# Moving the context stream's front and attention of the second block into the expert loop of layer 1

## The chip, the cores and the metric

The kernel runs on one core of a Trainium2 chip. The metric is device time in microseconds (us) of one execution. All arithmetic is fp32.

## The reference, cut to what matters

Two networks run one after the other on 256 tokens of width 1024.

```
first_block(x):   for layer in (0, 1):
    x += g1 * attention(norm(x))            # layer 0 differential, layer 1 stick-breaking
    x += g2 * moe(norm(x))                  # 32 experts of 1024 -> 512 -> 1024, top 2 of 8 in the top group
    then final norm
second_block(x, ctx):   y = ctx; for l in (0, 1):
    for each stream s in (y, x):            # context stream y, main stream x
        f, gate, u, v, gate, c_q, c_kv, k_rope, a_gate = split(norm_mod(s) @ w_in[l])   # 2208 columns
        fourier branch, spatial gate branch, low-rank q, k, v with norms of heads (rope for x)
    x += gate * (concat(f, g, attend(q_x, [k_y, k_x], [v_y, v_x]) * silu(a_x)) @ w_out[l])
    if l == 0:  y += gate_c * (concat(f, g, attend(q_y, k_y, v_y) * silu(a_y)) @ w_out[l])
```

The second block's context stream of layer 0 does not depend on the first block at all; only stream x does. The four passes of the second block are numbered p = 0 (context, l = 0), 1 (x, l = 0), 2 (context, l = 1, keys and values only), 3 (x, l = 1).

## The kernel before

Each engine has its own program, with the order written out by hand; semaphores tie them together.

**The ring.** Weights come through `ring`, six slots (`RING`) of 2 MB. Item n of one long list goes to slot n % 6. SyncE walks the list: it waits until the slot's earlier user is `free` and issues one transfer (L1318 to L1333; the last two experts in pieces, L1306 and L1311). For each expert these are gate, up and down, 2 MB each.

**The expert loop (`experts`, both layers).** For expert e TensorE computes gate and up of up to 64 gathered rows (32 instructions of 512 columns), then half of a gather for the quad of experts to come, waits for `hid`, turns it, does the second half of the gather, waits for `hidT` and computes `down` (16 instructions). ScalarE applies SiLU (L1643), frees gate and up, copies `hidT` (L1507), applies gain and shift to the gathered rows (L1591) and stores the result rows of the expert before. VectorE multiplies SiLU by up (L1928, `hid`) and scales `down`'s result (L1950, `out_ev`). PSUM banks 0 and 1 alternate for gate and up, 5 and 6 for `down`, 3 takes the gathers. At e = 28 (`TAIL`) every engine reads the fullest count and the last four experts' lists are turned; from there results are scattered by matmuls.

**What layer 1's loop already does for the context stream (p = 0).** Its rows are normed, turned at e = 3 and 4, and multiplied by the five sections of `w_in`, which come as ring items at e = 6, 11, 16, 21 and 26 (`Y0_AT`); each has two fills (one per tile of 128 tokens) into banks 4 and 7. Section "kv" is 160 columns wide, the other four are 512.

**The second block.** After the loop, `sp_second` on SyncE issues the first section for x, small weights and constants (L499, L531), further sections and the output weights (L528) into slots 0 and 1 in turn; slots 2 to 5 hold the second block's own tiles. TensorE (`pe_second`) turns x and works through 20 half fills of p = 1, and among them, by the list `X0_IN`, does the 15 steps of `front(0, j)` and the 20 of `attention(0, k)`. A front step is one of: turning the low-rank parts (`turn_c`), matmuls of a unit of q or k and v, turning a unit's heads, one of three Fourier steps, the spatial gate, turning the mixed parts. An attention step k computes scores of unit k (a head and a tile), turns the normed exponentials of unit k - 2, and every second step multiplies by v. ScalarE and VectorE have the same steps in the same order (copies, Sqrt, Exp; squares, norms, maxima). Then `Y0_OUT` goes through the output projection of p = 0 with `front(1, j)` among it.

Of the kernel before, what the change touches and what calls it, by code (L numbers as in the profile page):

```python
# [12 lines left out]

# [24 lines left out]
RING = 6  # L38
SLOT = KT * 512
# [93 lines left out]
def program(nc, a, out, sb, sem, ctx):  # L133
# [124 lines left out]
    y_rows = [h, carve(TT, D)]  # L258
# [3 lines left out]
    selw = work[:, 4416:5440].rearrange("p (e t k n) -> p e t k n", e=QUAD, t=TT, k=2)  # L262
# [24 lines left out]
    cut = Cut()  # L287
    g4, g4b, g4c, og, eg = (cut(TT, NG) for _ in range(5))
    e32, e32b, memb, place, spot, fits, share, share2 = (cut(TT, NX) for _ in range(8))
# [3 lines left out]
    row_of, w12, kept = (cut(2, TT) for _ in range(3))  # L293
# [3 lines left out]
    EARLY = (2, 1)  # L297
    L_BASE = [4, 12 + 3 * NX - EARLY[0]]
# [20 lines left out]
    def down_done(eng, l, e):  # L319

        down = expert_item(l, e, 2)
        eng.wait_ge(*((sem("early_used"), EARLY[0] * l + e + 1) if e < EARLY[l] else (free(down), down // RING + 1)))

    def gu_bank(e):

        return bank[0 if e >= TAIL else e % 2]

    def slot(n):
        return n % RING

    def loaded(eng, n):

        eng.wait_ge(sem(f"loaded{slot(n)}"), 16 * (n // RING + (slot(n) >= 4)))

# [31 lines left out]
    Y0_AT = (6, 11, 16, 21, 26)  # L366
    Y0_BANKS = (4, 7)
    tail = ring[:, 2:RING, :].rearrange("p r n -> p (r n)")
    t_at = [0]

    def cut2(*shape):
        n = int(np.prod(shape))
        t = tail[:, t_at[0]:t_at[0] + n]
        t_at[0] += n
        assert t_at[0] <= (RING - 2) * SLOT
        names = "abc"[:len(shape)]
        return t if len(shape) == 1 else t.rearrange(f"p ({' '.join(names)}) -> p {' '.join(names)}",
                                                     **dict(zip(names[1:], shape[1:])))

    y = cut2(TT, D)  # L380
    cst2 = cut2(CONST2_W)
    w_uq, w_ukv, w_fm, w_gs = cut2(2, 768), cut2(1024), cut2(2, 256), cut2(4, P)
    qa_g, kva_g, qn_g, kn_g, ln_g = cut2(256), cut2(P), cut2(A_QK), cut2(A_QK), cut2(HD)
    kT2 = cut2(A_HEADS, 2 * S)
    scratch = cut2(4608)
    tok = [scratch[:, 768 * k:768 * k + 768].rearrange("p (h e) -> p h e", h=A_HEADS) for k in range(2)]
    sqr = scratch[:, 1536:2304].rearrange("p (h e) -> p h e", h=A_HEADS)
    rot = scratch[:, 2304:2560].rearrange("p (h e) -> p h e", h=A_HEADS)
    AT = scratch[:, 2560:3584].rearrange("p (k c s) -> p k c s", k=2, c=2)
    FT = scratch[:, 3584:4096].rearrange("p (c s) -> p c s", c=2)  # L390
# [6 lines left out]
    qT2 = carve(A_HEADS, S)  # L397
    v2 = carve(2 * TT, A_HEADS, A_V)
    mixT = [carve(4, S), carve(4, S)]
    assert carve.at <= y_turn_at  # L400
    carve = Carver(y_turn_at)
    hT2 = carve(KT, S)
    y_raw = hT2.rearrange("p a b -> p (a b)").rearrange("p (t d) -> p t d", t=TT)
    cqT = carve(2, S)
    ckvT = carve(S)
    out_tmp = carve(2, 512)
# [3 lines left out]
    for name, w in CONST2_COLS:  # L410
        C2[name] = cst2[:, at:at + w]
        at += w
# [82 lines left out]
    X1_IN = share_steps([0] * 11 + [1, 1, 1, 1, 2, 2, 2, 1, 4])  # L495

    def small_weights(eng, l, name):

        put = lambda dst, src, s_: eng.dma_start(dst, src).then_inc(sem(s_), 16)  # L499
        put(w_uq, a["w_uq_2"][l].rearrange("(c p) n -> p c n", p=P), name)  # L500
        put(w_ukv, a["w_ukv_2"][l], name)
        put(w_fm, a["w_fmix_2"][l].rearrange("(c p) n -> p c n", p=P), name)
        put(w_gs, a["g_ws_2"][l].rearrange("h p q -> p h q"), name)
# [5 lines left out]
    def small_in(eng, p):  # L509

        eng.wait_ge(*((sem("pool_weights"), 128 + 160) if p >= 2 else (sem("small_in"), 176)))
# [6 lines left out]
    def sp_second(sp):  # L518
        last = expert_item(1, NX - 1, 2)
        sp.wait_ge(free(last), last // RING + 1)  # L520
        for r, (p, what) in enumerate(WEIGHTS2):
# [35 lines left out]
    def pool_second(pool):  # L557
        pool.wait_ge(sem("x_done"), 4)
        mod_row(pool, rows[:, 4, :], 0, 2, "gate_y_in")
        pool.wait_ge(sem("x_fin"), TT)  # L560
        mod_row(pool, rows[:, 3, :], 1, 2, "gate_x_in")
        pool.wait_ge(sem("h2"), every("h2", 1))
        norm_rows(pool, 2)
        pool.wait_ge(sem("f_out"), every("f_out", 1))
# [52 lines left out]
    def keep_warm(b, n):  # L617

        for _ in range(n):
            nc.tensor.matmul(bank[b][:, 0:S], ident, cst[:, 0:S], start=True, stop=True, skip_group_check=True)  # L620
# [13 lines left out]
    def take_turned(act, copy, p, ts, banks):  # L634

        for t in ts[::2]:
            act.wait_ge(sem("h2T_mm"), nth("h2T_mm", p, t // 2 + 1))
            if p % 2:
                gain, shift, _ = col_set[4 + p // 2]
                for k in (t, t + 1):  # L640
                    nc.scalar.activation(hT2[:, k, :], bank[banks[t // 2]][:, k % 2 * S:(k % 2 + 1) * S], ACT.Identity,
                                         scale=gain[:, k:k + 1], bias=shift[:, k:k + 1]).then_inc(sem("h2T"), 1)
# [118 lines left out]
    def act_second(act, link, copy):  # L761
# [88 lines left out]
        for t in range(TT):  # L850
            stream_rms(act, link, 1, t)
# [1585 lines left out]
```

## Time and profile before

| | us |
|---|---|
| median of 3 runs | 1889.09 |
| lowest, highest | 1888.32, 1898.73 |
| the profiled execution's own time | 1889.08 |
| its span, first to last instruction | 1887.3 |
| TensorE busy in the span | 1699.9 (90%) |
| mean granted TensorE clock | 0.964 of full speed |
| HBM read and written | 572.83 MB and 12.15 MB |

The profile is of one execution. Its time is compared with the median, and instants are us from the span's start. A busy TensorE row is not TensorE at its peak: matmuls overlap, and their ends are modelled, so the distance between starts is the better measure.

### The profile page before, as it was taken

Reading aid. Unit: us, or ns where it says so; the run is one execution under the profiler, and the core shown is the slowest. Engines: PE = TensorE matmul, PEld = TensorE weight load, DVE = VectorE, ACT = ScalarE, POOL = GpSimd, SP = SyncE. Lnnn points to the kernel's source line nnn. Section 1 sums busy time; section 2 is a strip of 40 time slices with the busy share of each in tenths; the row PEclk is TensorE's granted clock in tenths of the full one; section 3 lists DMA queues with packets and bytes.
Section 4 is the critical chain, followed back from the end, with each engine's and each line's share of the span. In section 5 each row is a group of like instructions: output and inputs, shape, how many; then the busy total and the mean of one; then the engine's idle time right before and its main releaser. Section 6 shows DMA issues by size and latency. Waiting matters only on the chain.

```text
span 1887.3 us, 18240 instructions
## 1 busy us (share of the span) xinstructions
PE 1699.9 (90%) x7421; PEld 848.5 (45%) x7421; DVE 489.5 (26%) x927; ACT 405.8 (22%) x909; POOL 96.1 (5%) x167
## 2 busy tenths in 40 slices
PE   5997999888988879989999899999989899899988
PEld 3833543333333325735544333333443556555564
DVE  1356210000001104234240000000102334653362
ACT  2025221111101102025221111011111334443351
POOL 1121000000000010122000000000000000100000
PEclk9998999999999989989999999999999899999999
DMA  9999379999999999987379999999998712213310
GB/s 350 360 356 397 143 279 424 423 423 422 422 422 421 422 416 398 347 335 240 148 273 421 422 420 422 419 416 416 418 419 344 272 59 90 86 64 114 123 57 23
DMA packets 122519, 586.30 MB, mean 311 GB/s; under 512 B 10290, under 2 KB 15482, under 8 KB 97848
## 3 DMA queue, kind: packets, MB, share of 16 engines
q1 hardware_dynamic: 99064, 491.94, 64.6%
q0 software_dynamic: 16192, 82.06, 11.7%
q10 hardware_dynamic: 7168, 11.02, 1.6%
q8 instruction: 62, 1.02, 0.2%
q14 instruction: 33, 0.27, 0.0%
HBM read 572.83 MB, written 12.15 MB: 310 GB/s over the span
## 4 chain that ended last, share of the span: by engine, by line
PE 58%; DMA 27%; DVE 6%; ACT 3%; SPq 3%; issue 3%; ACTq 0%; DVEq 0%
PE psum L2029 53%; DMA ring<-in_expert_w_up 21%; DMA ring<-in_diff_w_in 2%; DMA work<-in_ada_w 2%; SPq L1306 1%; PE psum L620 1%; DMA ring<-in_consts 1%; DMA work<-in_w_mod 1%; DVE small L967 1%; SPq L1327 1%; PE psum L2268 1%; PE psum L1097 1%; DVE work L1928 1%; DVE work L1720 1%; ACT work L1643 1%
## 5 line engine op out<-in xcount | busy, mean ns | idle before, releaser
L2029 PE MATMUL psum<-ring,work 128*64 128x512 f32 (+5 forms) x4432 | 1154.8, 576 | 78.1 <-DMA ring<-in_expert_w_up 63.6
L2029 PEld LDWEIGHTS psum<-ring,work 128*64 128x64 f32 (+2 forms) x4432 | 445.0, 153 | 703.2 <-issue 667.1
L2029 PE MATMUL psum<-work 128*128 128x192 f32 (+8 forms) x920 | 192.5, 376 | 6.9 <-DVE small L1780 2.2
L1928 DVE TENSOR_TENSOR work<-work,psum 128x256 f32<-128x256 f32 x64 | 27.0, 421 | 611.6 <-ACT work L1643 611.6
L2029 PEld LDWEIGHTS psum<-work 128*128 128x128 f32 (+2 forms) x920 | 130.7, 192 | 101.0 <-issue 80.9
L1643 ACT ACTIVATE work<-psum 128x256 f32<-128x256 f32 x64 | 24.6, 385 | 688.5 <-PE psum L2029 688.5
L2029 PE MATMUL psum<-work,ring 128*128 128x256 f32 (+1 forms) x728 | 161.2, 380 | 4.4 <-DMA ring<-in_diff_w_in 1.5
L2029 PEld LDWEIGHTS psum<-work,ring 128*128 128x128 f32 x728 | 136.0, 192 | 29.7 <-issue 7.1
L1507 ACT ACTIVATE work<-psum 128x256 f32<-128x256 f32 (+4 forms) x165 | 70.3, 439 | 222.1 <-PE psum L2029 69.1
L1950 DVE TENSOR_TENSOR work<-psum,rows 128x512 f32<-128x512 f32 x64 | 44.3, 692 | 272.1 <-PE psum L2029 272.0
L1720 DVE SCALAR_TENSOR_TENSOR work<-work,small 128x2048 f32<-128x2048 f32 x28 | 65.9, 2352 | 79.3 <-DMA work<-in_ada_w 78.8
L1507 ACT ACTIVATE ring<-psum 128x512 f32<-128x512 f32 (+3 forms) x82 | 49.9, 609 | 76.8 <-PE psum L2029 56.4
L1591 ACT ACTIVATE work<-psum,small 128x192 f32<-128x192 f32 x128 | 58.5, 507 | 23.7 <-PE psum L2029 23.7
L1469 POOL DMA_INDIRECT work<-expert_rows,picks x8 | 7.7, 963 | 882.1 <-DMA expert_rows<-work 880.3
L2268 PE MATMUL psum<-cst,work 128*128 128x128 f32 x128 | 28.0, 300 | 16.1 <-DVE work L1928 16.1
L620 PE MATMUL psum<-cst 128*128 128x256 f32 x166 | 42.0, 406 | 0.0
L967 DVE TENSOR_REDUCE small<-psum 128x1 f32<-128x512 f32 (+1 forms) x48 | 28.8, 600 | 47.4 <-PE psum L2029 47.2
L2029 PE MATMUL psum<-work,small 128*2 128x512 f32 (+1 forms) x256 | 37.3, 666 | 3.8 <-DMA work<-in_ada_w 2.0
L840 ACT ACTIVATE ring<-psum,small 128x512 f32<-128x512 f32 (+1 forms) x48 | 29.6, 617 | 41.8 <-DVE small L967 40.2
L1177 PE MATMUL psum<-cst,ring 128*128 128x128 f32 x160 | 27.3, 286 | 11.9 <-DVE ring L973 11.4
L620 PEld LDWEIGHTS psum<-cst 128*128 128x128 f32 x166 | 32.7, 204 | 11.4 <-issue 7.0
L2029 PE MATMUL psum<-work,cst 128*128 128x256 f32 (+4 forms) x152 | 26.9, 400 | 12.1 <-DVE work L1999 6.3
(256 smaller groups left out, 815.1 us busy)
## 6 DMA issues: line engine op xcount, KB each, us to landing
ring<-in_expert_w_gate SPq DMA_DIRECT2D x60, 2048.0 KB, 17.0
ring<-in_expert_w_up SPq DMA_DIRECT2D x60, 2048.0 KB, 21.2
ring<-in_expert_w_down SPq DMA_DIRECT2D x57, 2048.0 KB, 20.8
work<-in_ada_w POOLq DMA_DIRECT2D x40, 1024.0 KB, 8.0
ring<-in_w_in SPq DMA_DIRECT2D x12, 2048.0 KB, 9.0
work<-in_w_mod POOLq DMA_DIRECT2D x16, 1024.0 KB, 7.7
ring<-in_diff_w_in SPq DMA_DIRECT2D x6, 2048.0 KB, 38.1
ring<-in_sb_w_in SPq DMA_DIRECT2D x6, 2048.0 KB, 25.3
```

Source lines behind the costliest of these rows:

```text
L620: nc.tensor.matmul(bank[b][:, 0:S], ident, cst[:, 0:S], start=True, stop=True, skip_group_check=True)
L840: nc.scalar.activation(pe_[:, k % 3, 0:n * P], bank[4 + k % 3][:, 0:n * P], ACT.Exp, bias=nm2[:, k % 3:k % 3 + 1], accum_out=sm2[:, k % 4: ...
L967: V.tensor_reduce(nm2[:, k % 3:k % 3 + 1], bank[4 + k % 3][:, 0:n * P], AX.X, ALU.max, negate=True).then_inc(sem("a_max"), 1)
L1177: ins = T.transpose(bank[(7, 2)[u % 2]][:, j * P:(j + 1) * P], pe_[:, u % 3, j * P:(j + 1) * P], ident)
L1507: copy = lambda o_, i_: nc.scalar.activation(o_, i_, ACT.Copy)
L1591: ins = nc.scalar.activation(hS[:, c // QUAD % 2, t, 0:QUAD * LIST], bank[b][:, k * S:k * S + QUAD * LIST], ACT.Identity, scale=gain[:, t: ...
L1643: nc.scalar.activation(s_act, gu_bank(e)[:, 0:S], ACT.Silu).then_inc(sem("silu"), 1)
L1720: ins = V.scalar_tensor_tensor(now, now, cond[:, 0, t:t + 1], before, ALU.mult, ALU.add)
L1928: V.tensor_tensor(hid, s_act, gu_bank(e)[:, S:2 * S], ALU.mult).then_inc(sem("hid"), 1)
L1950: V.tensor_tensor(outb[:, e % 2, :], bank[5 + e % 2], gate2, ALU.mult).then_inc(sem("out_ev"), 1)
L2029: return T.matmul(out_, lhsT, rhs, start=start, stop=stop, skip_group_check=True)
L2268: ins = T.transpose(bank[2][:, j * P:(j + 1) * P], src[:, j * P:(j + 1) * P], ident)
```

## The change

- All 15 front steps and 20 attention steps of p = 0 leave the second block's first stage, and run in layer 1's expert loop from e = 9 on: one ahead of an expert's gate and up, one after its first half gather. On ScalarE and VectorE they stand at the matching places. For this the five sections come one after another at e = 4 to 8, and the turning of the context rows at e = 2 and 3.
- From expert 7 on the ring has five slots in turn, not six (`KEPT` = 1). The sixth holds the second block's small weights and constants, which POOL now loads in the loop once the slot is free, and not SyncE after it.
- PSUM: in layer 1 gate and up use bank 0 alone, `down` bank 5 alone (to e = 27), gathers bank 1; `down` of expert e waits for the scaling of e - 1. The steps use 3, 4, 6 and 7.
- The SiLU table is loaded again ahead of SiLU in each expert that may have steps (`y0_roots`).
- Tiles get other places; keys and values of the two streams are apart, so the scores of x are two matmuls of 256 columns, not one of 512.

```
+KEPT = 1
-    Y0_AT = (6, 11, 16, 21, 26)
+    Y0_AT = (4, 5, 6, 7, 8)
+    SPLIT_AT = 7
+    SPLIT = expert_item(1, SPLIT_AT, 0)
-    def gu_bank(e):
-        return bank[0 if e >= TAIL else e % 2]
+    def gu_bank(l, e):
+        return bank[0 if l or e >= TAIL else e % 2]
+    def down_bank(l, e):
+        return 5 + (0 if l and e < TAIL else e % 2)
     def slot(n):
-        return n % RING
+        return n % RING if n < SPLIT else (n - SPLIT) % (RING - KEPT)
+    def turn_of(n):
+        return sum(slot(m) == slot(n) for m in range(n))
-    FRONT = 15
-    X0_IN = share_steps([0, 1, 1, 1, 1, 1, 2, 2, 2, 2, 2, 3, 3, 3, 3, 3, 1, 1, 1, 1])
+    FRONT, ATTN = 15, 20
+    Y0_STEP0 = Y0_AT[-1] + 1
+    def y0_step(front, attention, e, half):
+        j = 2 * (e - Y0_STEP0) + half - 1
+        if 0 <= j < FRONT:
+            front(0, j)
+        elif FRONT <= j < FRONT + ATTN:
+            attention(0, j - FRONT)
+    def y0_roots(e):
+        return 0 <= 2 * (e - Y0_STEP0) < FRONT + ATTN + 2
...
 (sp_second)
             if r == 0:
-                small_weights(sp, 0, "small_in")
-                sp.dma_start(cst2, a["consts2"]).then_inc(sem("small_in"), 16)
+                mix_weights(sp, 1, "small_x")
...
 (pe_second; act_second and dve_second alike)
-        for n, js in enumerate(X0_IN):
+        for n in range(2 * len(fills(1))):
             in_half(1, n)
-            for j in js:
-                front(0, j) if j < FRONT else attention(0, j - FRONT)
...
 (gpsimd)
+                for n in range(SPLIT - RING, SPLIT):
+                    if slot(n) >= RING - KEPT:
+                        pool.wait_ge(free(n), turn_of(n) + 1)
+                small_weights(pool, 0, "small_in")
+                pool.dma_start(rope, a["consts2"][:, 0:ROPE_W]).then_inc(sem("small_in"), 16)
+                pool.dma_start(cst2, a["consts2"][:, ROPE_W:]).then_inc(sem("small_in"), 16)
...
 (scalar, experts)
+                if l:
+                    y0_step(front, attention, e, 0)
+                    if y0_roots(e):
+                        act.preload_act_table(ACT.Silu)
                 act.wait_ge(sem("gu"), EACH["gu"] * l + e + 1)
...
                 if 0 < e < TAIL:
                     store(l, e - 1)
+                if l and e == Y0_AT[-1]:
+                    c_root(act, link, 0)
+                    v_root(act, 0)
+                if l:
+                    y0_step(front, attention, e, 1)
...
 (vector, experts: half 0 ahead of the wait for SiLU, half 1 ahead of the scaling)
...
 (tensor, experts)
+                if l:
+                    y0_step(front, attention, e, 0)
                 if i == 0:
                     pe.wait_ge(sem("hS"), EACH["hS"] * l + QUAD * (q + 1))
...
-                    gather(sel[:, (q + 1) % 2], 2 * i, bank[3][:, 0:QUAD * LIST])
+                    gather(sel[:, (q + 1) % 2], 2 * i, bank[GATHER[l]][:, 0:QUAD * LIST])
+                if l:
+                    y0_step(front, attention, e, 1)
                 pe.wait_ge(sem("hid"), EACH["hid"] * l + e + 1)
...
-                if e >= 2:
+                if l and 0 < e <= TAIL:
+                    pe.wait_ge(sem("out_ev"), EACH["out_ev"] * l + e)
+                elif e >= 2:
                     pe.wait_ge(sem("out_ev"), EACH["out_ev"] * l + e - 1)
```

## Rows read from the trace of the kernel before

**Rows 1.** The page: busy time of each engine, share of the span, instructions.

```profile
PE 1699.9 (90%) x7421; PEld 848.5 (45%) x7421; DVE 489.5 (26%) x927; ACT 405.8 (22%) x909; POOL 96.1 (5%) x167
```

**Rows 2.** Windows: length, busy PE, PEld, DVE, ACT, POOL, granted clock, DMA share, GB/s.

```profile
963.78:1029.41 65.63, 64.29 (x308) 25.44 (x308) 15.59 (x18) 10.58 (x25) 0.00 (x0) 1.00 0.97 392
...
1109.94:1192.04 82.10, 78.11 (x323) 30.68 (x323) 6.03 (x11) 9.95 (x25) 0.00 (x0) 0.98 1.02 419
1192.04:1276.34 84.30, 79.12 (x323) 30.97 (x323) 6.03 (x11) 9.61 (x22) 0.00 (x0) 0.96 1.02 420
1276.34:1356.06 79.72, 76.24 (x323) 30.14 (x323) 7.66 (x14) 9.95 (x24) 0.00 (x0) 1.00 1.01 415
...
1473.16:1589.53 116.37, 104.44 (x435) 66.20 (x436) 37.67 (x92) 47.52 (x103) 0.10 (x1) 0.94 0.34 118
```

**Rows 3.** Timeline, ScalarE: SiLU of experts 3, 10, 11, 12, 27, 28, 31.

```profile
1002.95 0.38 ACT L1643 ACTIVATE work<-psum 128x256 f32<-128x256 f32 x1 [6.33 <-PE psum L2029]
...
1109.94 0.39 ACT L1643 ACTIVATE work<-psum 128x256 f32<-128x256 f32 x1 [14.22 <-PE psum L2029]
...
1136.66 0.38 ACT L1643 ACTIVATE work<-psum 128x256 f32<-128x256 f32 x1 [6.38 <-PE psum L2029]
...
1149.30 0.38 ACT L1643 ACTIVATE work<-psum 128x256 f32<-128x256 f32 x1 [9.70 <-PE psum L2029]
...
1395.49 0.38 ACT L1643 ACTIVATE work<-psum 128x256 f32<-128x256 f32 x1 [9.70 <-PE psum L2029]
...
1414.41 0.38 ACT L1643 ACTIVATE work<-psum 128x256 f32<-128x256 f32 x1 [3.90 <-PE psum L2029]
...
1454.72 0.38 ACT L1643 ACTIVATE work<-psum 128x256 f32<-128x256 f32 x1 [11.91 <-PE psum L2029]
```

**Rows 4.** Waits of TensorE, 1029.40 to 1454.72: total, times, longest.

```profile
PE psum L2029 <- DMA ring<-in_expert_w_up: 17.9, 9, 3.9
```

**Rows 5.** Timeline in the loop: narrow fills, last scaled rows, a wide section's two fills.

```profile
1034.90 4.37 PEld L2029 LDWEIGHTS psum<-ring,work 128*128 128x128 f32 x32 [0.81 <-issue]
...
1358.49 0.50 ACT L1591 ACTIVATE work<-psum,small 128x192 f32<-128x192 f32 x1
...
1361.56 14.08 PE L2029 MATMUL psum<-work,ring 128*128 128x256 f32 x64
```

**Rows 6.** Timeline after the loop: SyncE's issue of the first section, VectorE's wait.

```profile
1460.98 0.55 SPq L528 DMA_DIRECT2D ring<-in_w_in  x1
...
1485.90 0.18 DVE L714 RECIPROCAL small<-small 128x4 f32<-128x4 f32 x1 [14.50 <-DMA ring<-in_consts]
```

**Rows 7.** Waits of TensorE in the second block's first stage, 1473 to 1590.

```profile
PE psum L1067 <- DVE work L719: 7.6, 1, 7.6
PE psum L1177 <- DVE ring L973: 4.0, 5, 2.1
PE psum L2029 <- DVE work L980: 0.4, 1, 0.4
```

**Rows 8.** Timeline, TensorE: three fills without a step among them.

```profile
1743.48 20.77 PE L2029 MATMUL psum<-ring,work 128*128 128x512 f32 x48
```

**Rows 9.** The chain that ended last: start, length; a wait for output weights.

```profile
1690.67 7.64 DMA ring<-in_w_out
```

**Rows 10.** Timeline, ScalarE: a copy, a table load, Exp, its sum, a copy.

```profile
1563.27 0.60 ACT L671 ACTIVATE work<-psum 128x512 f32<-128x512 f32 x1 [1.08 <-PE psum L2029]
...
1563.88 1.28 ACT L840 ACT_TABLE_LOAD   x1
...
1565.18 0.47 ACT L840 ACTIVATE ring<-psum,small 128x256 f32<-128x256 f32 x1
1565.55 0.19 ACT L840 ACTIVATION_READ_ACCUMULATOR ring<-psum,small 128x1 f32 x1
1565.64 0.37 ACT L1507 ACTIVATE ring<-psum 128x256 f32<-128x256 f32 x1
```

**Rows 11.** Groups by form, VectorE, 1485 to 1590: count, busy, mean ns.

```profile
L910 DVE TENSOR_TENSOR ring<-ring,small 128x768 f32<-128x768 f32 x4 | 3.8, 958 | 0.1
```

More of the change, by code:

```diff
@@ L14 @@
+from collections import namedtuple
 from contextlib import ExitStack
@@ L287, in program @@
     cut = Cut()
+    place, share = cut(TT, NX), cut(TT, NX)
+    w12 = cut(2, TT)
+    rt_free = y_turn_at + TT * D + S + cut.at
     g4, g4b, g4c, og, eg = (cut(TT, NG) for _ in range(5))
-    e32, e32b, memb, place, spot, fits, share, share2 = (cut(TT, NX) for _ in range(8))
+    e32, e32b, memb, spot, fits, share2 = (cut(TT, NX) for _ in range(6))
     hot = cut(2, TT, NX)
@@ L292, in program @@
     gm, pm, gs, m1, m2, ex, den = (cut(TT) for _ in range(7))
-    row_of, w12, kept = (cut(2, TT) for _ in range(3))
+    row_of, kept = (cut(2, TT) for _ in range(2))
     w1, w2 = w12[:, 0, :], w12[:, 1, :]
@@ new lines, in program @@
+    cut2 = Cut2(RING - KEPT, KEPT)
+    ROPE_W = 2 * TT * A_ROPE
+    cst2 = cut2(CONST2_W - ROPE_W)
+    w_uq, w_ukv = cut2(2, 768), cut2(1024)
+    assert cut2.at <= KEPT * SLOT
+    wsT = cst[:, P:5 * P].rearrange("p (h q) -> p h q", h=4)
+    gains, at = [], 7 * P + SLOTS
+    for w in (256, P, A_QK, A_QK, HD, ROPE_W):
+        gains.append(cst[:, at:at + w])
+        at += w
+    qa_g, kva_g, qn_g, kn_g, ln_g, rope = gains
+    assert at <= 13 * P + SLOTS
+    mix_y = rows[:, 3, :].rearrange("p (c s) -> p c s", c=4)
@@ L846, in attention, with act_second @@
                     act.wait_ge(sem("a_pv"), nth("a_pv", p, u // 2 - 1))
[L847 removed]
+                copy(space(p).pT[:, u % 4, 0:n, :], bank[space(p).back[u % 2]][:, 0:n * P].rearrange("p (k q) -> p k q", k=n)).then_inc(
                     sem("a_pT"), 1)
+        return take_c, take_unit, unit_root, unit_turned, front, attention
+    def act_second(act, link, copy):
+        take_c, take_unit, unit_root, unit_turned, front, attention = act_steps(act, link, copy)
         for t in range(TT):
@@ L852, in act_second @@
         take_turned(act, copy, 1, range(KT), (2, 3, 4, 5))
-        for n, js in enumerate(X0_IN):
-            if n % 2:
-                take_fill(act, link, copy, 1, n // 2, n // 2 % 2)
-            for j in js:
-                front(0, j) if j < FRONT else attention(0, j - FRONT)
+        for n in range(len(fills(1))):
+            take_fill(act, link, copy, 1, n, n % 2)
         c_root(act, link, 1)
@@ L1057, in turn_c @@
             pe.wait_ge(sem("c_n"), nth("c_n", p, TT))
+            if p in (1, 2):
+                pe.wait_ge(sem("a_pT"), every("a_pT", p - 1))
+                pe.wait_ge(sem("a_o"), every("a_o", p - 1))
             if p:
@@ L1338, in overflow @@
             last = expert_item(l, TAIL - 1, 2)
-            for n in range(last - RING + 1, last + 1):
-                sp.wait_ge(free(n), n // RING + 1)
+            for n in range(last - RING + l * KEPT + 1, last + 1):
+                sp.wait_ge(free(n), turn_of(n) + 1)
             for e in range(NX):
@@ L1618, in experts @@
         def experts(l):
+            front, attention = act_steps(act, link, copy)[4:]
             act.preload_act_table(ACT.Silu)
@@ L2351, in experts @@
                     if l:
-                        pe.wait_ge(sem("proj"), every("proj", 0))
-                    turn_tail()
+                        pe.wait_ge(sem("a_pT"), every("a_pT", 0))
+                        pe.wait_ge(sem("a_o"), every("a_o", 0))
+                    turn_tail(l)
+                if l:
+                    y0_step(front, attention, e, 0)
                 if i == 0:
```

299 lines of the change are left out of this document (172 added, 127 removed).

## The prediction

> **What bounds the kernel now.** I went from the page to the stages, then to single waits. The page [rows 1] says 90% TensorE over the span, an average over stages with different limits. The windows [rows 2] separate them. In layer 1's expert loop the DMA engines are busy all the time and move 415 to 420 GB/s, while TensorE has gaps; TensorE's waits for expert weights add up to 17.9 us [rows 4]. The reader is to see that both are nearly the bound: between two starts of SiLU without a wait lie 12.64 us (e = 11 to 12), with a context fill of 512 columns 26.72 us (e = 10 to 11) [rows 3], so a fill costs TensorE 14.08 us, as its own row says [rows 5]. Five experts and a fill are 77.3 us of TensorE; the window of the same five (e = 10 to 15) lasts 82.1 us, the next two 84.3 and 79.7 [rows 2]. Three windows, 246.1 us, hold 48 weight items of 2 MB: 5.13 us an item with the result rows that are stored beside them, 15.4 us an expert. So this loop is paced by transfers, with TensorE 1 us an expert below them. In the second block's first stage (1473.16 to 1589.53) it is the reverse: DMA 34% busy, TensorE the bound, with waits of its own [rows 2, 7].
>
> Notation: s(e) is the start of SiLU for expert e; the windows [rows 2] are cut at s(0), s(5), s(10), s(15), s(20), s(25) and at the stage's ends. s(0) = 963.78, s(3) = 1002.95, s(31) = 1454.72 [rows 2, 3].
>
> **The change, part by part.**
>
> *1. The five context sections move from e = 6, 11, 16, 21, 26 to 4, 5, 6, 7, 8.* Nothing is added, but five transfers and fills now lie together. TensorE: the transposes of the context rows come one expert earlier, so s(3) = 1002.95 + 1.2 = 1004.1; the narrow section is 4.4 us (32 weight loads in 4.37 us [rows 5]), so s(4) = 1004.1 + 12.64 + 4.4 = 1021.2; the four others give s(8) = 1021.2 + 4 x 26.72 = 1128.1. In these experts the transfers want 15.4 + 5.0 = 20.4 us and TensorE 26.7. The ring can only fill up; then the DMA engines idle. That is the price of the change: idle of a resource that paced the whole loop. Before, s(10) is 1109.94 [rows 3]; with this it comes near 1157 (1128.1 + 2 x 12.64 + 4 us of steps).
>
> *2. Two steps per expert, e = 9 to 26.* What do the 35 steps cost TensorE? In the stage where they run now: 116.4 us [rows 2], less 12.0 us of waits (7.6 + 4.0 + 0.4) [rows 7], less the fills of stream x. Fills: 96 instructions of 512 columns at 20.77/48 = 0.43 us [rows 8] are 41.5, 64 of 256 at 14.08/64 = 0.22 are 14.1, 32 of 160 are 4.4 [rows 5]: 60.0 us. Left are 44.4 us for the steps with all their seams. By instruction counts the 15 front steps are near 24 of it (the widest a good 3 us), the 20 of attention near 20: 1.0 us each. That they fit between an expert's matmuls without more is to be bounded: below, a step hides the 0.3 us that TensorE waits for `hid`, -0.2 us a step; above, another seam and wait of up to 1 us a step, as the wait for DVE L980 or L973 is 0.4 to 0.8 on average [rows 7]. I take zero, as steps sat in the same way between half fills.
>
> The path of TensorE: s(9) = 1140.7; to s(17) eight experts and 24 + 2 us of steps: 1140.7 + 101.1 + 26 = 1267.8. In attention an expert is 12.64 + 2 x 1.0 = 14.7 us, below the 15.4 of the transfers, so they catch up. TensorE alone would reach s(31) = 1267.8 + 9 x 14.7 + 5 x 12.64 + 6.3 = 1469.6 (6.3 is what e = 28 has above 12.64, from s(27) and s(28) [rows 3]).
>
> *3. Five slots from expert 7 on.* With a full ring TensorE is ahead of nothing: at s(17) the slots of gate and up come free and two transfers start, the third follows after `down`. First data after 7.64 - 5.0 = 2.6 us (a transfer alone took 7.64 us [rows 9]), three items 15.4: weights for e = 19 have landed 18 us after s(17), so s(19) may be 18 + 7.1 = 25 us after it, against 30.8 in transfer pace. The transfers' credit is therefore 5.7 us; a sixth slot would hold 5 more. s(31) by the transfers = 1267.8 + 14 x 15.4 - 5.7 = 1477.7. The later of the two paths decides: **s(31) = 1478, 23 us later than now.** The extra 6.3 us at e = 28 fits into the 2.8 us of slack per expert of the last four.
>
> *4. SiLU, Exp and Sqrt in turn on ScalarE.* Up to two table loads an expert, 19 times. One took 1.28 us and the Exp began 0.02 us after it [rows 10]. In the second half of an expert ScalarE ends the gains of the gathered rows 2.9 us after SiLU (1358.49 + 0.50 against s(25) = 1356.06) [rows 2, 5]; with about 1.0 us of step ahead of it, a table load, Exp with its sum 0.66 and copy 0.37 [rows 10] its step ends at 6.3 us. TensorE needs this copy only after `down`, 5.5 + 1.0 = 6.5 us after SiLU. Cost zero, but with 0.2 us of room. In the first half all of it lies beside 7.1 us of gate and up. If this cover is gone, TensorE pays the difference nine times. The Trainium skill, ScalarE: Activation LUTs, section What ACT_TABLE_LOAD costs, adds a drain of about 1.38 us to each load. The row shows none: the instruction ahead ends at 1563.87, the load starts at 1563.88 [rows 10]. By that rule nine steps would wait 1.2 us each, and as transfers pace these experts most of it would still be hidden.
>
> *5. VectorE.* Its longest step is two squares-and-sums and a norm, four operations of 0.96 us [rows 11], 4 us. Behind it in its queue are `hid` (first half) and the scaling of `down`'s result (second half), on which `down` of the next expert now waits, since bank 5 alone is left. Gate and up take 7.1 us, so `hid` isn't late; the scaling has until the next `down`, over 7 us. Zero. Single banks 0 and 5 have the same cover.
>
> *6. Small weights and constants through POOL at expert 7, 2.8 MB in 12 transfers.* At 420 GB/s that is 6.9 us of transfers, but in a stretch where the DMA engines idle: between 0 and 7 us, I take 0. Needed at e = 9, 30 us later. The final gain row, gate rows and squares move too: each has at least 10 us before its user, zero. Ahead of s(31) + 18.44 us (where the fills of x begin, 1473.16 - 1454.72) nothing is in the way: w_in was issued at 1460.98 [rows 6] and remains first.
>
> *7. What the second block loses.* The stage is 116.4 us. The steps go (44.4), and all the waits (12.0): 7.6 of them was TensorE behind VectorE L714, which waited 14.5 us for the constants [rows 6]. 60.0 us of fills remain. What is late next: the first output weights are issued when section `a` is used, and now only the 4.4 us of the narrow section cover the 7.64 us that this transfer takes alone [rows 9]: 3.2 us. Before, steps covered it. New stage 63.2 us, gain 53.2 us. The scores of stream x are now two matmuls of 256 columns in place of one of 512, 32 times: same columns, 0 to 0.1 us each, taken as 0.
>
> **Sum.** Span 1887.3 + 23.3 - 53.2 = 1857.4; with the 1.8 us between this execution's span and its time (1889.08, the median is 1889.09) 1859 us. Of 53 us of relief, the loop takes back 23.
>
> **Rivals.**
> *A, the loop takes back nothing (1836 us).* If transfers had idle room elsewhere, s(31) would stay. For it: TensorE alone would manage. Against it: share 1.01 to 1.02 in every window [rows 2]. 5%.
> *B, steps cost more than in the old stage (1875 us, up to 1886).* Mechanism: the seams of a step among expert matmuls, or ScalarE's chain of part 4. At 0.5 us a step, TensorE, 15.7 us an expert, stays above the transfers until e = 26: s(31) = 1469.6 + 35 x 0.5 = 1487; at 1 us it is 1505. Against 1478 that is 9 to 27 us more: 1868 to 1886, middle 1875. For it: the room of 0.2 us. Against it: the seams of the old stage are in the 44.4. 20%.
> *C, the other side: five slots let the transfers run dry (1917 us).* Place: e = 9 to 31. When the third item of an expert is issued only after `down`, and the queue is empty by then, each expert pays the 2.6 us before first data: 22 x 2.6 = 57 us, 1859 + 58 = 1917. It decides where work in flight at SiLU is less than the 6.5 us to the end of `down`. For it: one slot in six is gone. Against it: in transfer pace, at SiLU 7.1 us of the 15.4 ahead are done, 8 us are left, and two items of 10 us are added. 7%.
>
> **How the numbers follow.** My forecast has 68%. Its own spread: 15.2 to 15.6 us an expert (3 us either way), credit 0 to 11 us, the wait in part 7 between 0 and 5, small weights up to 7: 1851 to 1868. With most of B the range is 1850 to 1882; A and C and the top of B stay out. A measurement of this kernel can tell about 1% from no change: 1870.2 and 1908.0. Faster: forecast but for its edge, A, a little of B: 0.71. Same: most of B and the edge: 0.22. Slower: 0.07.
>
> **What the next profile would show.** Right: s(8) near 1128, 26.7 us apart for e = 5 to 8, DMA share down to 0.8 there; s(17) near 1268; 15.4 us an expert with short waits for w_up after about e = 20; s(31) near 1478; x fills in 60 us without a gap and a wait of some 3 us for w_out. Wrong: TensorE waits for `a_pT` or `a_n` in attention (B); DMA share well below 1 at e = 20 to 30 with waits for weights at once (C); s(8) early (A). The prediction fails if a step's price in its new place is not the old one, as TensorE has 0.7 us an expert to spare.

## The result, and the profile of the changed kernel

Median 1868.03 us (1867.41 to 1870.53, 4 runs), against 1888.7 us (1885.53 to 1898.73, 4 runs) of the kernel before on the same chip: ratio 0.9884, 95% interval 0.9846 to 0.9922. The forecast was 1859, with a range of 1850 to 1882; the median lies at the upper edge of the forecast's own spread, 1851 to 1868. The profiled execution took 1867.41 us with a span of 1865.4; my sum for the span was 1857.4. So 8.0 us have to be found, and they can be placed: 5.1 ahead of the second block, 3.1 behind its first stage and 0.1 in it (8.3, less the 0.3 by which I had rounded 1477.7 to 1478).

The page after, busy time as in [rows 1]:

```profile
PE 1686.7 (90%) x7485; PEld 859.5 (46%) x7485; DVE 488.3 (26%) x927; ACT 436.8 (23%) x933; POOL 102.7 (6%) x179
```

The share of TensorE is 90% as before, so the page alone tells nothing. The timeline of ScalarE does; these are SiLU of experts 0, 8, 9, 17, 25 and 31 (L1754 is L1643 of before), as in [rows 3]:

```profile
962.76 0.38 ACT L1754 ACTIVATE work<-psum 128x256 f32<-128x256 f32 x1 [7.35 <-PE psum L2152]
...
1127.36 0.38 ACT L1754 ACTIVATE work<-psum 128x256 f32<-128x256 f32 x1 [6.58 <-PE psum L2152]
...
1140.01 0.38 ACT L1754 ACTIVATE work<-psum 128x256 f32<-128x256 f32 x1 [4.84 <-PE psum L2152]
...
1264.96 0.38 ACT L1754 ACTIVATE work<-psum 128x256 f32<-128x256 f32 x1 [6.93 <-PE psum L2152]
...
1387.90 0.38 ACT L1754 ACTIVATE work<-psum 128x256 f32<-128x256 f32 x1 [7.48 <-PE psum L2152]
...
1482.84 0.38 ACT L1754 ACTIVATE work<-psum 128x256 f32<-128x256 f32 x1 [11.09 <-PE psum L2152]
```

| | forecast | measured |
|---|---|---|
| s(8) | 1128.1 | 1127.36 |
| s(17) | 1267.8 | 1264.96 |
| s(31) | 1478 (1477.7) | 1482.84 |
| s(31) to the first fill of x | 18.44 | 18.44 (1501.28) |
| fills of x | 60.0 | 59.6 |
| wait for the output weights | 3.2 | 3.68 |
| stage | 63.2 | 63.27 |

Up to s(17) the forecast is 2.8 us too late, from there to s(31) it is 8.0 us too short (1477.7 - 1267.8 = 209.9, measured 217.88). Of the 2.8 us, 1.0 lies ahead of s(0), which came at 962.76 and not at 963.78; from s(0) to s(31) the forecast was 513.9 us and the loop took 520.08. The windows, columns as in [rows 2], show which engine sets the pace where:

```profile
1020.43:1127.36 106.93, 105.95 (x393) 48.87 (x393) 4.92 (x9) 12.17 (x28) 7.09 (x12) 1.00 0.92 352
...
1140.01:1264.96 124.95, 122.80 (x583) 55.75 (x583) 30.50 (x48) 42.38 (x71) 0.00 (x0) 1.00 1.01 414
1264.96:1387.90 122.94, 116.04 (x581) 53.01 (x581) 25.09 (x74) 46.63 (x93) 0.00 (x0) 0.99 1.01 422
1387.90:1482.84 94.94, 80.27 (x360) 30.67 (x361) 11.42 (x22) 11.36 (x23) 6.09 (x8) 0.96 1.01 412
```

In the first window, the four wide sections from s(4) to s(8), TensorE is busy all the time and the DMA engines move 352 GB/s; in the other three they move 412 to 422 at a share of 1.01. From s(9) to s(17), the front steps, TensorE is busy 122.8 of 124.95 us: both resources are full there, up to s(14) without any gap on TensorE (81.17 of 81.17 us). From s(17) on TensorE waits, mostly for `up`. As in [rows 4], 1127 to 1483:

```profile
PE psum L2152 <- DMA ring<-in_expert_w_up: 14.0, 11, 2.1
...
PE psum L2152 <- DMA ring<-in_expert_w_gate: 2.9, 2, 2.1
```

The first of these waits of over 1 us is at e = 17, where nothing of the two steps' own waits, `a_n` or `a_pT`, shows; this is the end of a chain of transfers:

```profile
1250.64 0.82 PE L2152 MATMUL psum<-work 128*128 128x192 f32 x4
1251.38 3.65 PE L2152 MATMUL psum<-ring,work 128*64 128x512 f32 x16
1254.97 0.70 PE L2152 MATMUL psum<-work,rows 96*128 96x256 f32 x2
1257.67 7.09 PE L2152 MATMUL psum<-ring,work 128*64 128x512 f32 x32 [2.00 <-DMA ring<-in_expert_w_up]
```

The reader is to see `down` (16 instructions), one score step, 2.0 us of nothing, then gate and up. The stage behind the loop is as it was drawn up, three kinds of fill without a step and then a wait:

```profile
1501.28 41.44 PE L2152 MATMUL psum<-ring,work 128*128 128x512 f32 x96
1542.55 13.98 PE L2152 MATMUL psum<-work,ring 128*128 128x256 f32 x64
1556.36 4.51 PE L2152 MATMUL psum<-ring,work 128*128 128x160 f32 x32
1564.55 5.25 PE L2152 MATMUL psum<-ring,rows 128*128 128x512 f32 x8 [3.68 <-issue]
```

From its end (1564.55) to the end of the span are 300.85 us, where before there were 297.77 (1887.3 - 1589.53). The windows of the wait and of the 2.45 us behind it, and of the first scores of stream x at p = 3, show most of why:

```profile
1560.87:1564.55 3.68, 0.00 (x1) 0.03 (x1) 3.10 (x7) 2.18 (x4) 0.00 (x0) 0.97 1.05 383
1564.55:1567.00 2.45, 2.45 (x3) 1.15 (x4) 2.31 (x5) 0.30 (x1) 0.00 (x0) 0.50 1.00 380
...
1797.00:1799.50 2.50, 2.50 (x7) 1.94 (x7) 0.71 (x2) 0.99 (x3) 0.00 (x0) 0.50 0.00 2
```

TensorE stood still for 3.68 us, and its granted clock was 0.50, that is 1.2 GHz, in the stretch after it. The three output halves up to the next instruction of another kind last 12.12 us; before, three such halves lasted 10.71 (windows 1564.55:1576.67 here and 1589.53:1600.24 of before): 1.4 us. Another 1.4 us are lost in the first score matmuls at p = 3, again at 0.50: eight records of 256 columns took 3.40 us (from 1796.06), four of 512 before 1.97 (from 1819.30). That leaves 0.3 of the 3.1 us unplaced.

### The profile page after: what moved, and what is told of

The parts are those of the page before. It is cut to its first block, busy times and chain, and to the rows that moved or that the text cites. A ratio compares the mean times of both kernels' runs of the same rounds, so it can differ in the third digit from the quotient of the medians.

```text
span 1865.4 us, 18398 instructions
## 1 busy us (share of the span) xinstructions
PE 1686.7 (90%) x7485; PEld 859.5 (46%) x7485; DVE 488.3 (26%) x927; ACT 436.8 (23%) x933; POOL 102.7 (6%) x179
## 3 DMA queue, kind: packets, MB, share of 16 engines
q8 instruction: 63, 1.03, 0.2%
## 4 chain that ended last, share of the span: by engine, by line
PE 59%; DMA 27%; DVE 6%; ACT 3%; issue 3%; SPq 2%; ACTq 0%; DVEq 0%
PE psum L2152 54%; DMA ring<-in_expert_w_up 18%; DMA work<-in_ada_w 3%; DMA ring<-in_diff_w_in 2%; DMA ring<-in_expert_w_gate 2%; PE psum L692 2%; SPq L1404 1%; DVE work L1834 1%; DMA work<-in_w_mod 1%; DVE small L1045 1%; PE psum L2391 1%; PE psum L1181 1%; ACT ring L1613 0%; DVE work L2120 0%; DMA ring<-in_w_out 0%
## 5 line engine op out<-in xcount | busy, mean ns | idle before, releaser
L2152 PE MATMUL psum<-ring,work 128*64 128x512 f32 (+5 forms) x4272 | 1095.4, 575 | 76.0 <-DMA ring<-in_expert_w_up 60.6
L2152 PEld LDWEIGHTS psum<-ring,work 128*64 128x64 f32 (+2 forms) x4272 | 424.6, 152 | 675.0 <-issue 639.5
L2152 PE MATMUL psum<-work 128*128 128x192 f32 (+9 forms) x1048 | 218.2, 371 | 8.9 <-DVE small L1894 2.2
L2152 PEld LDWEIGHTS psum<-work 128*128 128x128 f32 (+3 forms) x1048 | 144.2, 189 | 106.9 <-issue 86.0
L1754 ACT ACTIVATE work<-psum 128x256 f32<-128x256 f32 x64 | 24.5, 383 | 607.0 <-PE psum L2152 607.0
L2152 PE MATMUL psum<-work,ring 128*128 128x256 f32 x704 | 155.6, 381 | 3.7 <-DMA ring<-in_diff_w_in 2.3
L1613 ACT ACTIVATE work<-psum 128x256 f32<-128x256 f32 (+5 forms) x184 | 79.3, 443 | 230.7 <-PE psum L2152 87.2
L1613 ACT ACTIVATE ring<-psum 128x512 f32<-128x512 f32 (+2 forms) x54 | 34.6, 640 | 64.3 <-PE psum L2152 39.5
L2152 PE MATMUL psum<-work,cst 128*128 128x128 f32 (+4 forms) x176 | 30.3, 385 | 13.9 <-DVE work L2122 6.2
L1474 POOL DMA_DIRECT2D work<-in_ada_w x40 | 22.7, 571 | 215.1 <-DVE work L1834 162.1
L2152 PEld LDWEIGHTS psum<-work,cst 128*128 128x128 f32 (+1 forms) x176 | 21.4, 173 | 22.8 <-DVE work L2122 8.5
```

Source lines behind the costliest of these rows:

```text
L1474: pool.dma_start(ada_in[:, i % 3, 512 * k:512 * (k + n)], src[:, c * 512:(c + n) * 512].rearrange("(p t) n -> p t n", t=KT)[:, t, :]).then ...
L1613: copy = lambda o_, i_: nc.scalar.activation(o_, i_, ACT.Copy)
L1754: nc.scalar.activation(s_act, gu_bank(l, e)[:, 0:S], ACT.Silu).then_inc(sem("silu"), 1)
L2152: return T.matmul(out_, lhsT, rhs, start=start, stop=stop, skip_group_check=True)
```

## The experiments

A total of a few runs hardly tells 5 us here: s(0), ahead of which the kernels of this study do nearly the same work, lies between 958.96 and 970.59 us. The length of a stretch does: from s(0) to s(31), after and the three kernels with its loop (9 to 11 below) took 520.08, 520.31, 519.67 and 520.57 us. From the first fill of x to the end, 364.12 us in after, the kernels with its second block lie between 362.2 and 364.1. So the lengths of stretches carry the verdicts, and the ratios are given beside them. "Loop" is s(0) to s(31): 490.94 us before, 520.08 after, 29.1 more.

**1. Sections bunched, nothing else.** The kernel before with

```
-    Y0_AT = (6, 11, 16, 21, 26)
+    Y0_AT = (4, 5, 6, 7, 8)
-                if l and e in (3, 4):          # turning of the context rows
+                if l and e in (2, 3):
```

> The kernel before with one part of the change: the five context sections at experts 4 to 8 (rows turned at 2 and 3), six slots, no step moved. Theory T (the loop's loss is idle of the DMA engines while TensorE does five fills in a row, and is not recovered since transfers pace the rest): s(8) near 1128, s(31) 18 to 21 us later than in the kernel before (1454.7), so 1473 to 1476, and the whole 18 to 21 us slower, near 1908, as nothing is saved after the loop. Rival S (the loop's loss comes from the steps put into it): s(31) within 5 us of 1454.7, time near 1890. Rival L (it comes from the lost sixth slot): the same as S.

Measured: 1906.4 us, ratio 1.0107 (1.0074 to 1.0140); loop 510.37, 19.4 us more than before. Its windows of the four wide sections (from 1.4 us ahead of s(4) on) and of the 22 experts after s(9):

```profile
1016.40:1124.73 108.33, 107.35 (x400) 49.23 (x397) 4.92 (x9) 12.19 (x28) 0.00 (x0) 1.00 0.88 343
1137.37:1470.48 333.11, 291.30 (x1278) 113.00 (x1279) 37.39 (x68) 35.37 (x84) 5.55 (x7) 0.95 1.01 420
```

In the first the DMA engines move 343 GB/s, not 420: 77 GB/s over 108.3 us are 8.3 MB, and 8.3 MB at 420 are 19.9 us. That is as much as the whole loss, and it is not made good: the experts behind it run at the transfers' rate. Bunching alone makes the kernel slower by 1%.

**2. Five slots on top of it.** Expert 7 begins with five slots in turn, the sixth stays unused:

```
+KEPT = 1
     def slot(n):
-        return n % RING
+        return n % RING if n < SPLIT else (n - SPLIT) % (RING - KEPT)
```

> As the run before, and from expert 7 on five slots in turn; slot 5 stays unused in the loop; no step moved. T: one item (5.1 to 5.5 us) less of lead at the moment when transfers become the bound, so s(31) near 1480 and time near 1913, 5 us above the run with six slots. L: 15 us or more above it. If the changed kernel's s(31), 1482.8, differs from this one's by no more than 3 us, the steps cost the loop nothing; S wants 20 us there.

Measured: 1912.94 us, ratio 1.0142 (1.0108 to 1.0175); loop 515.43, 5.1 us more than with six slots. From s(9) to s(31), and the same in three parts, cut at s(17) and s(25), to be laid beside those of after:

```profile
1136.22:1474.39 338.17, 294.04 (x1278) 114.85 (x1279) 37.39 (x68) 35.28 (x85) 5.55 (x7) 0.95 1.01 420
...
1136.22:1259.79 123.57, 106.83 (x465) 42.18 (x465) 9.83 (x18) 13.43 (x32) 0.00 (x0) 0.94 1.02 423
1259.79:1382.59 122.80, 107.65 (x465) 43.09 (x465) 11.47 (x21) 13.43 (x32) 0.00 (x0) 0.94 1.01 422
1382.59:1474.39 91.80, 79.56 (x350) 29.58 (x351) 16.09 (x29) 8.42 (x21) 5.55 (x7) 0.96 1.01 413
```

At 15.4 us an expert 22 experts are 338.8 us. Six slots stay 5.7 us below this (333.1), five 0.6. One slot is one item of 5.1 us of stock, once, and not a price for each expert.

**3. Five slots, sections as before**, from expert 8 on.

> The kernel before with only the five slots, from expert 8 on (there the slots' numbers go on without a jump); sections where they were, no step moved. T: a lead is smaller by one item once, 5 us, s(31) near 1460, time 1889 to 1895. L with a queue that runs dry in each expert: 2.6 us for each of 23 experts, near 1940. My forecast's part 3 took zero in transfer pace and 5 us for a full ring.

Measured: 1897.05 us, ratio 1.0045 (1.0027 to 1.0064, 10 runs); loop 499.94, 9.0 us more. That is more than the 5 to 6 of one item. The later wide sections are the likely reason, each filling the smaller ring so that the transfers stop: in the expert behind each of them (s(11) to s(12), s(16) to s(17), s(21) to s(22), s(26) to s(27)) the DMA share is 0.91 to 0.95 at 364 to 368 GB/s, before it was 1.00 to 1.03 at 406 to 428. In the 22 experts from s(9) on (1094.67 to 1463.93, 369.3 us) the rate is 406 GB/s, before it was 417 over 361.9 us (1092.78 to 1454.72). With sections already over at e = 8, as in after, no such expert comes later.

**4. The small weights loaded twice**, in after:

```
                 small_weights(pool, 0, "small_in")
+                pool.wait_ge(sem("small_in"), 160)
+                small_weights(pool, 0, "small_in")
```

> The changed kernel, with the second block's small weights (2.1 MB of the 2.8 MB, ten transfers) loaded a second time by POOL at expert 7, after the first load has landed; same tiles, same data. If these transfers lie in idle time of the DMA engines, as forecast: 1868, no change. If the transfers already pace the loop there: 2.1 MB at 420 GB/s, 5 us, up to 8 us if small rows move slower: 1873 to 1876, all of it in s(31).

Measured: 1871.69 us, ratio 0.9916 (0.9888 to 0.9945); loop 521.97, 1.9 us more for the second copy of 2.1 MB. That is the price of the second copy, not of the first: it was still landing behind s(8), where the DMA engines had no idle time left for it (share 1.03 from s(8) to s(9), in after 0.95). The `up` item that is issued 5.6 us behind s(8) landed after 17.5 us here. In after it landed after 12.4 us, and after 12.4 in run 2 too, which has no small weights in its loop. So the first copy delayed nothing that came behind it.

**5. Front units computed twice.** After, with the matmuls of four front steps of the context stream (e = 9 to 13) repeated:

```
-            for j in range(2):                       # unit_mm
+            for j in (0, 1) if p else (0, 1, 0, 1):
```

> After's kernel, with the matmuls of the four front units of the context stream (e = 9 to 13) done twice, about 8 us more of TensorE in four steps. Theory (in the experts with front steps TensorE is the bound or equal to the transfers, so a step's price counts in full): SiLU of expert 17 some 7 to 8.6 us later, and SiLU of the last expert by nearly the same, as transfers pace the rest: loop 526 to 529 us. Rival (TensorE has room there, as transfers pace the whole loop): 520 to 522.

Measured: 1877.28 us, ratio 0.9927 (0.9897 to 0.9957). s(9) to s(17) takes 131.83 us in place of 124.95, 6.9 more, and the loop 527.13, 7.0 more. Its two windows, s(9) to s(17) and to s(25):

```profile
1144.24:1276.07 131.83, 131.32 (x607) 59.82 (x606) 30.51 (x48) 42.30 (x70) 0.00 (x0) 1.00 0.95 390
1276.07:1399.28 123.21, 114.59 (x581) 52.87 (x581) 25.11 (x74) 46.70 (x94) 0.00 (x0) 1.00 1.01 422
```

The share of the DMA engines fell to 0.95 where TensorE became the bound. TensorE was busy for 8.5 us more (131.32 against 122.80). Up to s(14) that is paid in full: s(9) to s(14) took 89.75 us in place of 81.17. From s(14) to s(17) 1.7 us come back, 42.08 in place of 43.78, out of the waits that after has there. So four fifths are paid, and nothing of that is given back behind s(17).

**6. Scores computed twice.** The same for attention, 16 matmuls of 0.43 us more at e = 16 to 24:

```
-                for j in range(1 + s):               # attention
+                for j in (0, 1) if s else (0, 0):
```

> After's kernel, with each score matmul of the context stream's attention (e = 16 to 24, 16 of 256 columns) done twice, about 0.43 us each, 7 us in all. Theory (in attention transfers pace and TensorE has 0.7 to 1 us an expert of room): 0 to 2 us more, loop 520 to 522 us. Rival B of the prediction (steps of attention are on the path): loop 527 us.

Measured: 1869.01 us, ratio 0.9879 (0.9839 to 0.9918); loop 520.79, 0.7 us more for 6.9 us of work, and within 0.3 of a kernel with the loop of after (520.57). TensorE's waits for `up` fell from 14.0 to 9.2 us in the loop; the work went into them:

```profile
PE psum L2152 <- DMA ring<-in_expert_w_up: 9.2, 6, 2.2
```

**7. One more table load an expert.** A load of the Sqrt table that nobody uses, ahead of the second attention step, e = 17 to 24:

```
+                if l and 17 <= e <= 24:
+                    act.preload_act_table(ACT.Sqrt)
                 if l:
                     y0_step(front, attention, e, 1)
```

> After's kernel with one more table load (Sqrt, used by nothing) on ScalarE ahead of the second attention step of each expert from 17 to 24, 8 loads of 1.28 us. Theory (transfers pace these experts, TensorE has 0.7 us of room and ScalarE about 1 us): 0 to 3 us more, 1868 to 1871. Rival (ScalarE's chain is in the path, as in my rival B): 8 x 1.28 = 10 us more, 1878; with a drain of 1.38 us for each load as well it would be 1889.

Measured: 1872.89 us, ratio 0.9900 (0.9880 to 0.9921); loop 520.33 for 10.2 us of loads, no more than kernels without them take. ScalarE, SiLU to the copy of the turned exponentials at e = 22:

```profile
1347.99 0.38 ACT L1754 ACTIVATE work<-psum 128x256 f32<-128x256 f32 x1 [6.29 <-PE psum L2154]
...
1350.62 0.50 ACT L1697 ACTIVATE work<-psum,small 128x192 f32<-128x192 f32 x1
1351.14 1.28 ACT L1765 ACT_TABLE_LOAD   x1
1352.43 1.28 ACT L915 ACT_TABLE_LOAD   x1
1353.72 0.47 ACT L915 ACTIVATE work<-psum,small 128x256 f32<-128x256 f32 x1
...
1354.19 0.37 ACT L1613 ACTIVATE work<-psum 128x256 f32<-128x256 f32 x1
```

The copy ends 6.6 us after SiLU, in after 5.3. TensorE now waits for it for 0.32 us ahead of the next transposes, and its wait for `gate` behind them is 0.35 us where it was 0.85 in after: what ScalarE costs, the transfers' slack takes.

**8. The last section one expert later**, at e = 9, and the steps at e = 10 to 27:

```
-    Y0_AT = (4, 5, 6, 7, 8)
+    Y0_AT = (4, 5, 6, 7, 9)
```

> After's kernel with the last context section at e = 9 in place of 8, and so the steps at e = 10 to 27. Theory (idle of the DMA engines while the sections are bunched is what the loop paid most for): one expert of 12.64 us of TensorE between two sections lets the transfers run 2 to 3 us more, SiLU of the last expert 3 us earlier, 1865 us. Rival (steps on TensorE set the end of the loop): the steps end an expert later, where TensorE has no slack left ahead of the last experts, 1868 to 1870.

Measured: 1869.6 us, ratio 0.9892 (0.9868 to 0.9915); loop 517.79, 2.3 us less. An expert without a section or step lets the transfers take up stock.

**9. The narrow section in fourth place** in the second block, so that `a`, 512 columns wide, covers the output weights:

```
-    ORDER = (..., ("gq", "gv", "f", "a", "kv"), ...)      # p = 1
+    ORDER = (..., ("gq", "gv", "f", "kv", "a"), ...)
```

> After's kernel, but in the second block's stage of stream x the section `a` (512 columns) is the last one and the narrow `kv` the fourth, so that the first output weights are issued ahead of a wide section. Theory (the lead of the output weights decides the wait of 3.7 us, and the clock of 0.50 that follows it comes from this wait): no wait, granted clock 1.00 at the first output matmuls; 1863 us, 4 to 5 us less than after. Rival 1 (the wait only moves, since some other section then arrives late): no gain, 1868. Rival 2 (the clock's fall has another cause): 1.4 us of the gain don't come, 1864.5.

Measured: 1874.14 us, ratio 0.9913 (0.9888 to 0.9939); from the first fill to the end 364.05 us, in after 364.12. My theory fell. It is even a little worse than it looks: the low clock at p = 3 did not come here, and the two kernels with the second block of after in which it did not come either (runs 4 and 6) took 363.3 and 362.2. TensorE, after 128 instructions of fills (the narrow one among them):

```profile
1509.35 45.78 PE L2152 MATMUL psum<-ring,work 128*128 128x512 f32 x128
1559.79 15.49 PE L2152 MATMUL psum<-work,ring 128*128 128x256 f32 x64 [4.65 <-DMA ring<-in_w_in]
```

The wait moved ahead of `a`, with the low clock behind it (15.49 us for a section of 13.98). With two slots in turn a transfer has one section as its cover; whatever stands behind the narrow one has 4.4 us.

**10. The narrow section first**, where nothing needs cover from it but a transfer that is issued together with its own:

```
+    ORDER = (..., ("kv", "gq", "gv", "f", "a"), ...)      # p = 1
```

> After's kernel with the narrow section `kv` as the first of stream x in the second block's first stage, so that every later transfer of the stage, the output weights too, is issued ahead of a wide section of 14 us. The lesson of the run with `kv` in fourth place: the wait sits behind the narrow section, wherever that stands, since with two slots each transfer has the section ahead as its only cover. Theory: no wait of over 1 us in the stage, clock 1.00 at the first output matmuls, from the first fill to the end 359 us in place of 364.1; 1863. Rival (the first sections then come late, or the front steps of x wait for `a`, now last): the 5 us come back as a wait at the start or after the stage, 1868.

Measured: 1865.69 us, ratio 0.9866 (0.9836 to 0.9896); from the first fill to the end 359.5 us, 4.6 less than after. About 1.4 of it is the low clock at p = 3, which did not come here; against runs 4 and 6, where it did not come either, it is 2.7 to 3.8 less. No wait ahead of the first output matmul, clock 1.00 there:

```profile
1502.40 47.00 PE L2152 MATMUL psum<-ring,work 128*128 128x160 f32 x128
1549.24 13.98 PE L2152 MATMUL psum<-work,ring 128*128 128x256 f32 x64
1563.06 3.60 PE L2152 MATMUL psum<-ring,rows 128*128 128x512 f32 x8
...
1571.03 3.70 PE L2152 MATMUL psum<-ring,rows 128*128 128x512 f32 x8 [0.94 <-DMA ring<-in_w_out]
```

**11. Matmuls of no use in the gap.** After, with 16 matmuls of 256 columns (`keep_warm(2, 16)`) between the last fill and the first output half.

> After's kernel with 16 matmuls of 256 columns of no use in the wait for the first output weights (3.5 us of work in a gap of 3.7 us). Theory (the granted clock fell to 0.50 because TensorE stood still): clock 1.00 in the first output matmuls, 1.4 us less, 1866.6. Rival (the clock falls there anyway, or the transfer is what is slow): 1868, and if the useless matmuls end later than the transfer, up to 1 us more.

Measured: 1872.77 us, ratio 0.9899 (0.9873 to 0.9925). I had the size wrong: they took 6.9 us, 0.43 each, and outlasted the transfer. But the mechanism shows, the first output half took 3.60 us in place of 5.25:

```profile
1567.05 7.07 PE L692 MATMUL psum<-cst 128*128 128x256 f32 x32
1573.95 3.60 PE L2153 MATMUL psum<-ring,rows 128*128 128x512 f32 x8
```

**12. 8 and 10 together.**

> Both changes that promise something at once: `kv` first in the second block, and the last context section at e = 9. If they add up, the loop from the first to the last SiLU is 517.8 us (as with the section at 9 alone) and the way from the first fill to the end 359 us: 7 us less than after, 1861.

Measured: 1864.17 us (1861.79 to 1872.03), ratio 0.9864 (0.9832 to 0.9897); loop 516.97, first fill to the end 360.8. It has the shortest profiled span of all kernels here, 1860.7 against 1865.4 of after. Its interval overlaps those of after and of 10: that it is better than after rests on the stretches, 3.1 and 3.3 us, not on the totals. The low clock at p = 3 came here as it did in after, so 3.3 us is a fair price for the order of the sections.

## Why the prediction was right, and where it was off

The direction and the main terms held: the second block's first stage gives 53.1 us (forecast 53.2), and the loop takes a good part of it back, 29.1 (forecast 23). The median lies 9.0 us above the forecast and within the range. Some luck is in that: the miss of 8.0 us from s(17) on was partly hidden by 1.0 us ahead of s(0) and 2.1 among the front steps that went the other way.

*Part 1, bunching: right.* s(8) was off by 0.7 us, counted from s(0) by 0.3 (164.60, forecast 164.3). Run 1 shows the price by itself, 19.4 us. I expected a DMA share of 0.8 there; it is 0.92 after and 0.88 in run 1, while the rate falls to 352 and 343 GB/s. In after the small weights lie in this window; run 2, with the same slots and without them, has 0.83 and 325 GB/s. The rate was the thing to predict, the share overstates what is moved.

*Part 2, the steps' TensorE: right in the mean, with the wrong spread.* An attention expert without a wait took 14.3 and 14.5 us (e = 18 to 19, 19 to 20), I had 14.7. s(9) to s(17) took 124.95 us, the wait of 2.0 among them, forecast 127.1: the front steps were cheaper than the 24 us. Runs 5 and 6 show what the sum needed and had no row for: in the front a microsecond of TensorE costs 0.8, in attention a tenth.

*Part 3, five slots and the credit: the step that failed.* "With a full ring TensorE is ahead of nothing", and so a credit of 5.7 us from s(17) on. The ring wasn't full at s(17). From s(9) on the DMA engines are busy throughout (share 1.01), so they never ran up against a full ring, and the first wait of 2.0 us comes before s(17), not after it. From s(17) on: 122.94 us for eight experts are 15.37 each, as the 15.4 said; the last six took 94.94, where 6 x 15.4 is 92.4, at 412 GB/s. With the credit of 5.7 gone, 2.5 more in the last six, 0.3 less in the eight, and 2.8 us less up to s(17), the sum is the 5.1 us between 1477.7 and 1482.84. The size of the credit was wrong as well, and run 2 shows it without any step: there the five slots did fill up (share 0.92 from s(8) to s(9)), and still they are only 0.6 us ahead of 15.4 an expert from s(9) on. 5.7 is what six slots gave (run 1); I had 5.7 for five and 5 more for the sixth.

*Loop as runs add it up:* bunching 19.4, the lost slot 5.1, and 4.6 between run 2 and after (520.08 - 515.43), 29.1 in all. Up to s(9) run 2 and after take the same time, 177.26 and 177.25 us. From there the windows differ by 1.4 us among the front steps, where TensorE is busy for 122.8 us in place of 106.8; by 0.1 in the attention experts; and by 3.1 in the last six, where only the last three steps are left. Something else moved into these six: POOL loads the final gain row (512 KB) at 1434.51, where the kernel before loaded it at 931.78, 32 us ahead of s(0). At 420 GB/s that is 1.2 us, an estimate; no run takes it out. The rest of the 3.1 is open. The six took 93.5 us in run 1, 91.8 in run 2, and 94.2 to 96.3 in after and runs 4 to 12. The rate of 412 GB/s there isn't due to the steps: runs 1 and 2 have 414 and 413.

*Part 4, table loads: right.* The load starts 0.02 us after the end of the instruction ahead. Run 7 bounds the whole part: eight more loads cost nothing that can be told. The Trainium skill, ScalarE: Activation LUTs, section What ACT_TABLE_LOAD costs, adds a drain to each load; here two loads in a row start 1.29 us apart and Exp 0.01 us after the second, so this trace disagrees.

*Part 5, VectorE, and single banks: right as far as the waits show.* TensorE's only waits for VectorE in the loop from s(8) on are for `hid`, 2.1 us in all. It wasn't tested by itself.

*Part 6, small weights: right for themselves, wrong for the final gain row.* The weights and constants that POOL loads at expert 7 cost nothing that can be seen: s(0) to s(9) as in run 2, and the item behind them lands as there. Run 4 prices a later copy, 1.9 us. The final gain row was taken at zero because its user comes late; but it now loads in a stretch that the transfers pace.

*Part 7, the second block: right to 0.1 us in the stage* (63.27), with the wait that was named as next; fills 0.4 us shorter and a wait 0.5 longer than forecast nearly cancel. Missed was its consequence, 1.4 us of low clock. The 1.4 us in the split scores at p = 3 look like a miss of "0 to 0.1 us each, taken as 0", but aren't: run 10 has the same matmuls at the full clock, 0.59 us a pair where after had 1.06, and there they cost what one of 512 columns cost.

*Rivals.* A, the loop takes nothing back: excluded by 29.1 us. B, dearer steps: excluded; TensorE's waits for ScalarE in the loop from s(8) on are 0.5 us in all, and runs 6 and 7 put extra work on both engines that B names for 0.7 and 0.3 us at most. The late 1868 is B's number by another cause. C, five slots run dry: excluded by run 2, 5.1 us in all against 2.6 an expert.

## What to carry to other kernels

Where two resources are nearly the bound, moving work into a loop costs nothing only in those iterations in which it falls into the other's waits: price each stretch by itself, and test it by doing the moved work twice. Work done twice is priced where the second copy runs: for a transfer that can be another stretch than the first copy's (run 4). Don't bunch the work of one engine in a loop paced by transfers: the ring's slots limit what the transfers can lay up, and idle of the pacing resource is not made good. When work that hid a transfer leaves a stage, look which transfer now has the shortest predecessor, and put the short one where its successor is already under way.

## What the hardware showed that I had not expected

- After 3.68 us of standstill TensorE's granted clock was 0.50 (1.2 GHz) in the 2.45 us behind it, and 1.4 us were lost; with useless matmuls in the gap it stayed at 1.00. At p = 3 it fell to 0.50 behind idle times of only 1.42, 1.02 and 0.78 us. The kernel before and run 10 have the same idle times there and kept 1.00. After, then run 10, first scores of stream x:

```profile
1791.13 1.16 PE L2152 MATMUL psum<-work,cst 128*128 128x128 f32 x8 [1.42 <-DVE work L831]
...
1796.06 0.82 PE L2152 MATMUL psum<-work 96*128 96x256 f32 x2 [0.78 <-ACT work L1613]
1796.67 1.06 PE L2152 MATMUL psum<-ring,work 96*128 96x256 f32 x2
1797.53 1.06 PE L2152 MATMUL psum<-work 96*128 96x256 f32 x2
```

```profile
1788.97 1.16 PE L2152 MATMUL psum<-work,cst 128*128 128x128 f32 x8 [1.41 <-DVE work L831]
...
1793.89 0.67 PE L2152 MATMUL psum<-work 96*128 96x256 f32 x2 [0.78 <-ACT work L1613]
1794.40 0.59 PE L2152 MATMUL psum<-ring,work 96*128 96x256 f32 x2
```

The fall came in after and runs 5, 7, 8, 11 and 12; it did not come in runs 4, 6, 9 and 10, nor in the four kernels without the steps in the loop (before, runs 1 to 3). So the change doesn't bring it each time, and that it has nothing to do with the change isn't shown either; what decides it stays open.
- The rate of the same weight stream differs by stretch at the same DMA share of 1.01: 422 GB/s in the attention experts, 414 in the front experts, 412 in the last six. In run 2, without steps, it was 423 in the stretch of the front experts, where after has TensorE busy nearly all the time; why the share stays at 1.01 there is open.
- The stretch ahead of s(0), nearly the same work in all kernels, varied by 11.6 us between executions, while the loop of after repeats to 0.9 us in four kernels. Why is open.
